# Two output products computed in pairs of chunks, with seven block products for eight in two steps of each pair

## The chip, the cores and the metric

The kernel runs on one core of one Trainium2 chip. The metric is the device time of one execution, in microseconds (us), as the median of several executions. The names used here: PE is TensorE (matmuls; PEld its weight loads), DVE is VectorE, ACT is ScalarE, POOL is GpSimd, SP is the engine whose queue issues the weight stream's transfers.

## What is computed

The reference is two transformer layers on 256 tokens of width 2048, all in float32. Only the two products that the change touches matter in detail:

```python
def hybrid_layer(x, ...):
    ...
    y = jax.nn.sigmoid(g_a) * y_a + jax.nn.sigmoid(g_b) * y_b
    return x + jnp.einsum('bsd,de->bse', y, w_out)          # first output product, 256x2048 by 2048x2048

def second_block(x, norm_mix_g, w_in, w_fourier, w_out, norm_mlp_g, w_up, w_down, norm_final_g):
    h = x
    u = _rmsnorm(h, norm_mix_g[layer])
    ...                                                      # Fourier mixing and attention give y_f and y_a
    y = jnp.concatenate([y_f, y_a], axis=-1)
    h = h + jnp.einsum('bse,ed->bsd', y, w_out[layer])       # second output product, the same size
    u = _rmsnorm(h, norm_mlp_g[layer])
    a = jnp.square(jax.nn.relu(jnp.einsum('bsd,df->bsf', u, w_up[layer])))
    h = h + jnp.einsum('bsf,fd->bsd', a, w_down[layer])
    return _rmsnorm(h, norm_final_g)
```

The results have to be close to float32, so every product is made from three matmuls in the chip's fp32r type: high part by high part, high by low, low by high.

## The kernel before

**The stream of weights.** All weights lie in one DRAM array, `stream`, in units of 128 by 2048 floats (1 MB). SP loads unit u into one of four places of `raw` as soon as the unit four back has been split. A unit is used in *pieces*. ACT rounds a piece to its high part (`w_hi`, L1154), DVE subtracts to get the low part (`w_lo`, L1665), PE multiplies with both. The places of `w_hi` and `w_lo` form a ring of four pieces (six in the last stage, the MLP). ACT and DVE run the same loop as PE: at position k (after PE has used piece k) they split piece k+4 into the freed place, and then do what else is written for position k, which the code calls its *slot*. So whatever stands in a slot on DVE delays the later splits and everything else behind it on that engine; each engine works its own list strictly in order, and engines meet only at semaphores.

**A plain product.** `project` (L593 to L595) makes one chunk, 512 columns of the result, for both halves of the tokens, in two PSUM banks: 8 pieces, 12 matmuls each. The two output products are four such chunks each: w_out from about 1017 to 1108 us, w_out_2 from about 1330 to 1422 us of the profile. After each chunk DVE adds the residual in `add_chunk` (L2202, results in `nat`).

**Turning.** The next stage needs the result with features on the partitions: for each of eight groups PE transposes four 128x128 blocks (L566) into a bank, ACT writes the high part (L1186), DVE the low part (L1709 with a norm's weight, L1705 without). The function `turn` places them: six groups (`tail`) after pieces 1 to 6 of the product's last chunk, one per piece, two (`head`) after pieces 2 and 3 of the next stage. Two banks alternate, so a group waits until DVE has read the group two before it.

**A pair with sums.** Other products (the pairs in the input stage, 160 to 458 us, and in the MLP) already use the scheme that the change brings here. `pair_in` works on two chunks at a time, so on four banks (`whole`), in eight steps of 2x2 blocks (two blocks of the inner dimension, two of the columns, times two halves of tokens). `plain_step` is 8 block products in two pieces. `sum_step` is 7 block products (the Winograd form of Strassen's scheme) in four pieces, and adds into four more banks (`mixed`). For it DVE makes sums of weight blocks ahead (`sum_weights`, L1679, L1682, L1683; this is done right after the first piece of the unit *before* the sum unit has been split) and sums of the activations' blocks once (`sum_x`, L1856 to L1862). The second `sum_step` of a pair is step 4 or 5 of 0 to 7. After the step behind it DVE joins the mixed banks: `join_mixed` part 0 in the first slot and part 1 in the second slot of that step (L1919 to L1924), then `join_whole` (L1936) as the last step's four products end. All eight banks are in use, so the next pair, whose `whole` is this pair's `mixed`, cannot start before `join_mixed` has ended; PE waits for `part_read`.

## Time and profile before

| what | us |
|---|---|
| median of 3 executions | 2123.62 (2123.57 to 2124.18) |
| the profiled execution | 2124.27 |
| its span, first to last instruction | 2122.4 |
| outside the span | 1.9 |
| PE busy | 2098.2 |
| DVE busy | 1447.1 |
| ACT busy | 1082.3 |

The granted TensorE clock was 1.00 in all stages shown below (2.4 GHz). A row of the timeline gives start, duration, engine, line, operation and tiles, and in brackets how long the engine idled before and what released it. "Matmuls are pipelined": a PE row's 0.39 us is a latency, and the pace is the distance of two starts.

### The profile page before, as it was taken

Reading aid. Unit: us, or ns where it says so; the run is one execution under the profiler, and the core shown is the slowest. Engines: PE = TensorE matmul, PEld = TensorE weight load, DVE = VectorE, ACT = ScalarE, POOL = GpSimd, SP = SyncE. Lnnn points to the kernel's source line nnn. Section 1 sums busy time; section 2 is a strip of 40 time slices with the busy share of each in tenths; the row PEclk is TensorE's granted clock in tenths of the full one; section 3 lists DMA queues with packets and bytes.
Section 4 is the critical chain, followed back from the end, with each engine's and each line's share of the span. In section 5 each row is a group of like instructions: output and inputs, shape, how many; then the busy total and the mean of one; then the engine's idle time right before and its main releaser. Section 6 shows DMA issues by size and latency. Waiting matters only on the chain.

```text
span 2122.4 us, 24939 instructions
## 1 busy us (share of the span) xinstructions
PE 2098.2 (99%) x10067; PEld 1752.8 (83%) x10067; DVE 1447.1 (68%) x1868; ACT 1082.3 (51%) x1392; POOL 37.9 (2%) x49
## 2 busy tenths in 40 slices
PE   8999999999999999999999999999999999999998
PEld 6888888888888877788888888888888888888886
DVE  5877788875555776556554455466896796797684
ACT  5545555555444674454455444355544554454553
POOL 0000000000000020000000000000000000000000
PEclk9999999999999999999999999999999999999999
DMA  7555555565465544355755442455555465546452
GB/s 266 184 181 196 199 189 208 185 248 181 178 223 189 188 154 156 122 220 197 296 188 184 180 170 107 142 207 187 193 202 186 172 224 193 180 187 227 180 218 98
DMA packets 56563, 402.60 MB, mean 190 GB/s; under 512 B 6240, under 2 KB 6496, under 8 KB 9216
## 3 DMA queue, kind: packets, MB, share of 16 engines
q1 hardware_dynamic: 53648, 380.67, 50.1%
q0 software_dynamic: 2656, 19.81, 2.4%
q8 instruction: 80, 1.31, 0.2%
q10 hardware_dynamic: 144, 0.52, 0.1%
q14 instruction: 35, 0.29, 0.0%
HBM read 392.59 MB, written 8.39 MB: 189 GB/s over the span
## 4 chain that ended last, share of the span: by engine, by line
PE 96%; DVE 1%; ACT 1%; issue 1%; DMA 0%; SPq 0%; POOLq 0%; POOL 0%; DVEq 0%; ACTq 0%
PE proj L593 15%; PE proj L595 15%; PE proj L594 15%; PE proj L1048 11%; PE proj L1051 6%; PE proj L698 4%; PE proj L699 4%; PE proj L700 4%; PE tbank L698 2%; PE tbank L699 2%; PE tbank L700 2%; PE tbank L566 2%; PE bank_a L698 1%; PE bank_a L700 1%; PE bank_a L699 1%; PE bank_b L698 1%
## 5 line engine op out<-in xcount | busy, mean ns | idle before, releaser
L1665 DVE TENSOR_TENSOR w_lo<-raw,w_hi 128x1024 fp32r<-128x1024 f32 x630 | 749.4, 1200 | 528.6 <-ACT w_hi L1154 521.5
L1154 ACT ACTIVATE w_hi<-raw 128x1024 fp32r<-128x1024 f32 x630 | 652.1, 1041 | 770.3 <-PE proj L595 495.1
L593 PE MATMUL proj<-w_hi,a_both 128*128 128x512 f32 x1280 | 512.2, 400 | 0.0
L595 PE MATMUL proj<-w_hi,a_both 128*128 128x512 f32 x1280 | 499.8, 390 | 0.0
L594 PE MATMUL proj<-w_lo,a_both 128*128 128x512 f32 x1280 | 498.4, 389 | 0.0
L595 PEld LDWEIGHTS proj<-w_hi,a_both 128*128 128x128 f32 x1280 | 240.2, 188 | 51.7
L593 PEld LDWEIGHTS proj<-w_hi,a_both 128*128 128x128 f32 x1280 | 240.5, 188 | 51.1 <-issue 4.3
L594 PEld LDWEIGHTS proj<-w_lo,a_both 128*128 128x128 f32 x1280 | 240.7, 188 | 47.5
L1048 PE MATMUL proj<-a_both,w_hi 128*128 128x512 f32 x672 | 168.4, 392 | 0.3 <-DVE a_both L1709 0.3
L1048 PEld LDWEIGHTS proj<-a_both,w_hi 128*128 128x128 f32 x672 | 121.0, 189 | 22.2 <-DVE a_both L1709 0.5
L1154 ACT ACTIVATE w_hi_deep<-raw 128x1024 fp32r<-128x1024 f32 x84 | 85.7, 1025 | 94.1 <-PE proj L1051 57.6
L1665 DVE TENSOR_TENSOR w_lo_deep<-raw,w_hi_deep 128x1024 fp32r<-128x1024 f32 x84 | 98.1, 1178 | 42.6 <-ACT w_hi_deep L1154 42.3
L1051 PEld LDWEIGHTS proj<-a_both,w_lo 128*128 128x128 f32 x672 | 91.7, 190 | 6.5
L1051 PE MATMUL proj<-a_both,w_lo 128*128 128x256 f32 x672 | 93.7, 282 | 0.0
L1048 PE MATMUL proj<-a_both,w_hi_deep 128*128 128x512 f32 x352 | 88.1, 392 | 0.0
L1048 PEld LDWEIGHTS proj<-a_both,w_hi_deep 128*128 128x128 f32 x352 | 63.4, 189 | 11.4
L698 PE MATMUL proj<-w_hi,a_both 128*128 128x512 f32 x164 | 64.0, 391 | 0.4 <-DVE w_lo L1665 0.4
L700 PE MATMUL proj<-w_hi,a_both 128*128 128x512 f32 x164 | 63.8, 389 | 0.0
L699 PE MATMUL proj<-w_lo,a_both 128*128 128x512 f32 x164 | 63.8, 389 | 0.0
L1051 PEld LDWEIGHTS proj<-a_both,w_lo_deep 128*128 128x128 f32 x352 | 48.0, 190 | 3.4
L1051 PE MATMUL proj<-a_both,w_lo_deep 128*128 128x256 f32 x352 | 49.1, 282 | 0.0
L593 PE MATMUL proj<-w_hi,lat_hi 128*128 128x512 f32 x112 | 45.6, 407 | 0.4 <-DVE v_b L2164 0.4
(511 smaller groups left out, 2997.0 us busy)
## 6 DMA issues: line engine op xcount, KB each, us to landing
raw<-stream SPq DMA_DIRECT2D x359, 1024.0 KB, 4.8
nat<-x SPq DMA_DIRECT2D x4, 512.0 KB, 9.0
z_store<-z POOLq DMA_DIRECT2D x1, 2048.0 KB, 8.2
ga_store<-z POOLq DMA_DIRECT2D x1, 2048.0 KB, 11.4
gb_store<-z POOLq DMA_DIRECT2D x4, 512.0 KB, 7.0
yb<-z_store POOLq DMA_DIRECT2D x4, 512.0 KB, 7.7
ga<-ga_store POOLq DMA_DIRECT2D x1, 2048.0 KB, 8.2
gb<-gb_store POOLq DMA_DIRECT2D x1, 2048.0 KB, 14.7
```

The source lines that it names most:

```text
L566: last = nc.tensor.transpose(tbank[tr.n % 2][:, b * P:(b + 1) * P], src(b), ident)
L593: nc.tensor.matmul(banks[t][:, :], ah, wh, start=first, stop=False)
L594: nc.tensor.matmul(banks[t][:, :], ah, wl, start=False, stop=False)
L595: last = nc.tensor.matmul(banks[t][:, :], al, wh, start=False, stop=end)
L698: nc.tensor.matmul(bank[:, :], hi, wh, start=first, stop=False)
L699: nc.tensor.matmul(bank[:, :], hi, wl, start=False, stop=False)
L700: return nc.tensor.matmul(bank[:, :], lo, wh, start=False, stop=end)
L1048: nc.tensor.matmul(banks[f], hi_places[s][:, cols], a_both[:, kt, :, :].rearrange("p s t -> p (s t)"), start=(kt == 0), stop=False)
L1051: last = nc.tensor.matmul(banks[f][:, 0:TOK], lo_places[s][:, cols], a_hi[:, kt, :], start=False, stop=(kt == KT - 1))
L1154: A(hi_places[s][:, 0:width], src, ACT.Copy).then_inc(w_rounded, 1)
L1665: V.tensor_tensor(lo_places[s][:, 0:width], src, hi_places[s][:, 0:width].bitcast(f32), SUB).then_inc(w_rest, 1)
```

## The change

Both output products are now two pairs of chunks each, numbered r = 0, 1 (w_out) and 2, 3 (w_out_2), each like `pair_in`: 8 steps, of which two are sum steps, at steps 3 and 5 (r=0), 2 and 5 (r=2), 1 and 4 (r=1 and 3). A pair has 20 pieces, numbered here 0 to 19 for the first pair of a stage and 20 to 39 for the second. The sum units of r=1 and r=3 are the second of the pair, so their weights' sums follow the split of piece 20, which falls on position 16 of the pair before.

- `sum_y` and `rest_of_y_sums` make the activations' sums in positions 0, 2, 3 and 5 of the stage, on DVE (ACT rounds them in `round_y_sums`).
- `add_mixed_out` is `join_mixed` with four additions more at the end of part 1 (the residual, all four tiles), and both parts stand in the two slots of the step behind the second sum step. `add_whole_out` adds the four whole banks and writes `nat`; `res_ready` counts these.
- The turning moves: PE's groups 0 to 3 come two by two after each piece of step 6 of the second pair, 4 and 5 after the pair, 6 and 7 after the next stage's first piece. They use two banks of the pair's `mixed` (`turn_banks`), so the first also waits for `add_mixed_out` part 1.
- The squares for the norm (`res_squares`, ACT) move with the results. The weights' units are laid out in the new order. The number of units is the same.

```diff
+            def pair_out(r, before, slot):                     # PE
+                whole, mixed = parts_out[r // 2][r % 2], parts_out[r // 2][1 - r % 2]
+                at, f = SUM_AT_OUT[r], r // 2
+                if r % 2:
+                    pe.wait_ge(part_read, READ_OUT + r)
...
+                for step in range(STEPS):
+                    g = ORDER_OUT[r][step]
+                    if step == at[0]:
+                        if r % 2:
+                            pe.wait_ge(res_ready, 8 * f + 4)
...
+                    if step in at:
+                        i = at.index(step)
+                        sum_step(2 * g, whole, mixed, a_hi, a_lo, yo_hi[f][:, i], yo_lo[f][:, i], 2 + 2 * f + i + 1, i == 0,
+                                 i == len(at) - 1)
+                    elif step == STEPS - 1:
+                        end_step(2 * g, whole, a_hi, a_lo, END_OUT)
+                    else:
+                        plain_step(...)
...
+            def turn_out(f):                                   # PE
+                def put(g):
+                    if not first:
+                        first.append(by_dve.n)
+                        pe.wait_ge(part_read, READ_OUT + 2 * f + 2)
+                    pe.wait_ge(res_ready, 8 * f + (4 if g < 4 else 6 if g < 6 else 8))
+                    group(from_nat(nat, g), by_dve, banks=turn_banks[f])
+                def tail(step, h):
+                    if step == 6:
+                        put(2 * h)
+                        put(2 * h + 1)
...
-            projection(y_head, y_before, r_tail)
+            pair_out(0, y_before, lambda step, h: y_head(2 + h) if step == 1 else None)
+            pair_out(1, None, r_tail)
+            r_put(4)
+            r_put(5)
...
-            projection(mix_slot, mix_before, m_tail)
+            pair_out(2, mix_before, lambda step, h: mix_slot(0) if step == 0 and h == 0 else None)
+            pair_out(3, None, m_tail)
+            m_put(4)
+            m_put(5)
...
+            def add_mixed_out(r, part):                        # DVE
+                if part == 0:
+                    dve.wait_ge(m_copied, PAIRS_IN + r + 1)
+                    chain(V.tensor_tensor(m[:, 2, :], mixed[2][:, :], m[:, 0, :], ADD))
+                    chain(V.tensor_tensor(m[:, 1, :], mixed[1][:, :], m[:, 2, :], ADD))
+                if part == 1:
+                    chain(V.tensor_tensor(m[:, 2, :], mixed[3][:, :], m[:, 2, :], ADD))
+                    V.tensor_tensor(m[:, 3, :], mixed[1][:, :], m[:, 2, :], ADD).then_inc(part_read, 1)
...
+                    for o in range(4):
+                        t, cols = part_out(r, o)
+                        last = V.tensor_tensor(m[:, o, :], other[:, t, cols], m[:, o, :], SUB if o in (1, 2) else ADD)
...
+            def pair_out(r, side):                             # DVE
+                    def slot(j):
+                        side(step, j)
+                        if r % 2 == 0:
+                            if (step, j) in ((0, 0), (1, 1)):
+                                sum_y(f, step)
+                            if (step, j) in ((1, 0), (2, 1)):
+                                rest_of_y_sums(f, step - 1)
+                        if step == at[-1] + 1:
+                            add_mixed_out(r, j)
+                        if r % 2 and step == 6:
+                            turned(f, 2 * j)
+                            turned(f, 2 * j + 1)
```

**Where the order of work changes.** First place: DVE at the start of the w_out product. The first row is the split of the stage's piece 3; L2188 to L2196 (L2301 to L2309 after) are the gating of the last chunk of the stage before. Before:

```order
L1665 TENSOR_TENSOR w_lo<-raw,w_hi 128x1024
L2188 TENSOR_TENSOR nat<-nat,stg 128x512 x2
L2193 TENSOR_TENSOR stg_126<-proj,stg_126 128x512
L2196 TENSOR_TENSOR nat<-nat,stg_126 128x512
L2193 TENSOR_TENSOR stg_126<-proj,stg_126 128x512
L2196 TENSOR_TENSOR nat<-nat,stg_126 128x512
L1665 TENSOR_TENSOR w_lo<-raw,w_hi 128x1024 x3
L1705 TENSOR_TENSOR a_both<-tbank,a_both 128x2x256
L1665 TENSOR_TENSOR w_lo<-raw,w_hi 128x1024
L1705 TENSOR_TENSOR a_both<-tbank,a_both 128x2x256
L1665 TENSOR_TENSOR w_lo<-raw,w_hi 128x1024 x4
```

After (from the last gating row on; L1792 to L1796 are the sums of weights, L2318 to L2329 those of the activations, `w_lo` is L1778 now):

```order
L2309 TENSOR_TENSOR nat<-nat,stg_134 128x512
L1778 TENSOR_TENSOR w_lo<-raw,w_hi 128x1024
L1792 TENSOR_TENSOR w_sum_mix<-raw 128x1024
L1795 TENSOR_TENSOR w_sum_mix<-w_sum_mix,raw 128x512
L1796 TENSOR_TENSOR w_sum_mix<-w_sum_mix,raw 128x512
L2318 TENSOR_TENSOR stg<-a_both 128x512
...
L1778 TENSOR_TENSOR w_lo<-raw,w_hi 128x1024 x2
L1818 TENSOR_TENSOR a_both<-tbank,a_both 128x2x256
L2329 TENSOR_TENSOR y_lo<-stg,y_hi 128x512
L1778 TENSOR_TENSOR w_lo<-raw,w_hi 128x512
L1818 TENSOR_TENSOR a_both<-tbank,a_both 128x2x256
L2318 TENSOR_TENSOR stg<-a_both 128x512
```

Between the splits of pieces 4, 5, 6 and 7 stand now three weight sums and twice the five operations of `sum_y`, where nothing stood but the low parts of two turned groups.

Second place: DVE at the change from r=0 to r=1 (the same stands at r=2 to r=3). Before, at the end of a chunk:

```order
L1705 TENSOR_TENSOR a_both<-tbank,a_both 128x2x256
L1665 TENSOR_TENSOR w_lo<-raw,w_hi 128x1024 x4
L2202 TENSOR_TENSOR nat<-proj,yb 128x512 x2
L1665 TENSOR_TENSOR w_lo<-raw,w_hi 128x1024 x8
L2202 TENSOR_TENSOR nat<-proj,yb 128x512 x2
```

After (the first row ends with piece 20, split in position 16; the row before the last is piece 22):

```order
L1778 TENSOR_TENSOR w_lo<-raw,w_hi 128x1024 x5
L1792 TENSOR_TENSOR w_sum_mix<-raw 128x1024
L1795 TENSOR_TENSOR w_sum_mix<-w_sum_mix,raw 128x512
L1796 TENSOR_TENSOR w_sum_mix<-w_sum_mix,raw 128x512
L2348 TENSOR_TENSOR added_mix<-tbank,added_mix 128x512
L2349 TENSOR_TENSOR added_mix<-proj,added_mix 128x512
L1778 TENSOR_TENSOR w_lo<-raw,w_hi 128x1024
L2351 TENSOR_TENSOR added_mix<-tbank,added_mix 128x512
L2352 TENSOR_TENSOR added_mix<-proj,added_mix 128x512
L2359 TENSOR_TENSOR added_mix<-yb,added_mix 128x512 x4
...
L1778 TENSOR_TENSOR w_lo<-raw,w_hi 128x1024
L1778 TENSOR_TENSOR w_lo<-raw,w_hi 128x512
```

Where lines are left out stand the four additions of the whole banks (L2371). Two additions between two chunks have become three weight sums, four joins, four residual additions and four additions of whole banks, with one split among them.

Third place: DVE at the turning, in the last chunk or pair of the product. Before, low parts come one group (two operations) per split:

```order
L1665 TENSOR_TENSOR w_lo<-raw,w_hi 128x1024 x2
L1709 SCALAR_TENSOR_TENSOR a_both<-tbank,par,a_both 128x256 x2
L1665 TENSOR_TENSOR w_lo<-raw,w_hi 128x1024
L1709 SCALAR_TENSOR_TENSOR a_both<-tbank,par,a_both 128x256 x2
L1665 TENSOR_TENSOR w_lo<-raw,w_hi 128x1024
```

After, they stand two by two behind the joins:

```order
L2348 TENSOR_TENSOR added_mix<-proj,added_mix 128x512
L2349 TENSOR_TENSOR added_mix<-bank_b,added_mix 128x512
L1778 TENSOR_TENSOR w_lo<-raw,w_hi 128x1024
L2351 TENSOR_TENSOR added_mix<-proj,added_mix 128x512
L2352 TENSOR_TENSOR added_mix<-bank_b,added_mix 128x512
L2359 TENSOR_TENSOR added_mix<-yb,added_mix 128x512 x4
L1778 TENSOR_TENSOR w_lo<-raw,w_hi 128x1024
L1822 SCALAR_TENSOR_TENSOR a_both<-bank_a,par,a_both 128x256 x2
L1822 SCALAR_TENSOR_TENSOR a_both<-bank_b,par,a_both 128x256 x2
```

The transposes moved from one group per piece to two per piece, and the joins stand ahead of them.

## Rows read from the trace of the kernel before

**Rows 1.** The page: busy us (share) and instructions of each engine
```profile
PE 2098.2 (99%) x10067; PEld 1752.8 (83%) x10067; DVE 1447.1 (68%) x1868; ACT 1082.3 (51%) x1392; POOL 37.9 (2%) x49
```

**Rows 2.** Busy us by window: PE, PEld, DVE, ACT, POOL, clock, DMA share, GB/s
```profile
372.00:415.00 43.00, 43.00 (x192) 35.59 (x191) 36.21 (x40) 22.98 (x25) 0.00 (x0) 1.00 0.54 199
1017.00:1108.00 91.00, 91.00 (x419) 75.27 (x417) 52.54 (x59) 44.18 (x60) 2.31 (x4) 1.00 0.66 252
1330.00:1422.00 92.00, 92.00 (x419) 76.20 (x418) 49.78 (x56) 43.94 (x59) 0.00 (x0) 1.00 0.49 172
```

**Rows 3.** Who waited for whom: total us, times, longest us
```profile
PE proj L698 <- DVE w_lo L1665: 0.4, 1, 0.4
...
PE proj L1048 <- DVE a_both L1709: 0.3, 1, 0.3
```

**Rows 4.** Timeline of PE in w_out_2 and in w_out: start us, duration us, engine, line
```profile
1334.48 0.40 PE L594 MATMUL proj<-w_lo,a_both 128*128 128x512 f32 x1
...
1402.04 0.39 PE L595 MATMUL proj<-w_hi,a_both 128*128 128x512 f32 x1
...
1025.48 0.60 PE L566 MATMUL tbank<-cst,nat 128*128 128x128 f32 x4
...
1028.70 0.60 PE L566 MATMUL tbank<-cst,nat 128*128 128x128 f32 x4
```

**Rows 5.** Timeline of DVE, a pair of the input stage, around a weight sum
```profile
307.41 1.23 DVE L1665 TENSOR_TENSOR w_lo<-raw,w_hi 128x1024 fp32r<-128x1024 f32 x1
308.55 1.22 DVE L1679 TENSOR_TENSOR w_sum_vo<-raw 128x1024 f32<-128x1024 f32 x1
...
311.14 2.96 DVE L1665 TENSOR_TENSOR w_lo<-raw,w_hi 128x1024 fp32r<-128x1024 f32 x3
```

**Rows 6.** Timeline of PE, the same pair, at its wait for that split
```profile
312.42 0.50 PE L698 MATMUL proj<-w_hi,a_both 128*128 128x512 f32 x1
312.75 0.39 PE L699 MATMUL proj<-w_lo,a_both 128*128 128x512 f32 x1
```

**Rows 7.** Timeline of ACT and of PE at the same pair's last step
```profile
325.67 1.06 ACT L1154 ACTIVATE w_hi<-raw 128x1024 fp32r<-128x1024 f32 x1 [1.11 <-PE proj L700]
...
325.47 0.39 PE L698 MATMUL proj<-w_hi,a_both 128*128 128x512 f32 x1
...
330.91 0.39 PE L698 MATMUL bank_a<-w_hi,a_both 128*128 128x512 f32 x1
```

**Rows 8.** Timeline of DVE, the same pair, its joins
```profile
325.25 0.68 DVE L1919 TENSOR_TENSOR joined<-tbank,joined 128x512 f32<-128x512 f32 x1
325.97 0.69 DVE L1920 TENSOR_TENSOR joined<-bank_b,joined 128x512 f32<-128x512 f32 x1
326.77 1.23 DVE L1665 TENSOR_TENSOR w_lo<-raw,w_hi 128x1024 fp32r<-128x1024 f32 x1
327.91 0.68 DVE L1923 TENSOR_TENSOR joined<-tbank,joined 128x512 f32<-128x512 f32 x1
328.63 0.69 DVE L1924 TENSOR_TENSOR joined<-bank_b,joined 128x512 f32<-128x512 f32 x1
329.42 2.49 DVE L1936 TENSOR_TENSOR joined<-proj,joined 128x512 f32<-128x512 f32 x4
```

**Rows 9.** Timeline of DVE, sums of the activations in the input stage
```profile
89.29 0.69 DVE L1856 TENSOR_TENSOR x_whole<-a_both 128x512 f32<-128x512 f32 x1
...
91.07 1.22 DVE L1665 TENSOR_TENSOR w_lo<-raw,w_hi 128x1024 fp32r<-128x1024 f32 x1
```

**Rows 10.** Timeline of DVE at the start of the w_out stage
```profile
1020.13 1.29 DVE L2188 TENSOR_TENSOR nat<-nat,stg 128x512 f32<-128x512 f32 x2
...
1023.99 2.35 DVE L1665 TENSOR_TENSOR w_lo<-raw,w_hi 128x1024 fp32r<-128x1024 f32 x2
```

**Rows 11.** Timeline of DVE: a turned group's low part; the last Fourier group's in w_out_2
```profile
1404.70 0.87 DVE L1709 SCALAR_TENSOR_TENSOR a_both<-tbank,par,a_both 128x256 fp32r<-128x256 f32 x2
...
1335.09 0.69 DVE L2267 TENSOR_TENSOR a_both<-bank_b,a_both 128x512 fp32r<-128x512 f32 x1
```

More of the change, by code:

```diff
@@ L59 @@
 SUM_UNITS = _sum_units()
-SUMS_IN = 2 * PAIRS_IN
 def _pieces():
@@ L1474, in res_squares @@
                     square_sum(stg2[:, t, :], nat[:, t, c * CW:(c + 1) * CW], ss2[:, t, c:c + 1])
-            for c in range(4):
-                def slot(j, c=c):
-                    if c == 0:
-                        turn_head(j)
-                    if c == 3:
-                        turn_tail(j, "mix_g")
-                    if c and j == 3:
-                        res_squares(c - 1, 2 * c)
-                pieces(slot=slot)
-                chunk.add()
+            pair_out(0, lambda step, j: turn_head(2 + j) if step == 1 else None)
+            pair_out(1, lambda step, j: None)
             for i in range(4):
@@ L1553, in _ @@
                     mapped(g)
-            for c in range(4):
-                def slot(j, c=c):
-                    if c == 0 and j == 0:
-                        mapped(FG - 1)
-                    if c == 3:
-                        turn_tail(j, "mlp_g")
-                    if c and j == 3:
-                        res_squares(c - 1, 8 + 2 * c)
-                pieces(slot=slot)
-                chunk.add()
+            pair_out(2, lambda step, j: mapped(FG - 1) if step == 0 and j == 0 else None)
+            pair_out(3, lambda step, j: None)
             def round_hidden(c):
@@ new lines, in pair_out, with slot @@
+            def pair_out(r, side):
+                at, f = SUM_AT_OUT[r], r // 2
+                for step in range(STEPS):
+                    def slot(j):
+                        side(step, j)
+                        if r % 2 == 0:
+                            if (step, j) in ((0, 0), (1, 1)):
[5 more added lines that the diff above has]
+                        if r % 2 and step == 6:
+                            turned(f, 2 * j)
+                            turned(f, 2 * j + 1)
+                        if r % 2 and step == 7 and j == 0:
+                            turned(f, 4)
+                            turned(f, 5)
+                    if step == STEPS - 1:
+                        add_whole_out(r)
+                    pieces(4 if step in at else 2, slot=slot)
+                chunk.add(2)
@@ L2215, in mean_of_chunks @@
+            pair_out(0, lambda step, j: turn_head(2 + j) if step == 1 else None)
+            pair_out(1, lambda step, j: None)
             def mean_of_chunks(n):
@@ L2285, in _ @@
                     mapped(g)
-            for c in range(4):
-                pieces(slot=(lambda j: mapped(FG - 1) if j == 0 else None) if c == 0 else
-                       (lambda j: turn_tail(j, "mlp_g")) if c == 3 else None)
-                add_chunk(c, nat)
+            pair_out(2, lambda step, j: mapped(FG - 1) if step == 0 and j == 0 else None)
+            pair_out(3, lambda step, j: None)
             def rest_of_hidden(c):
```

205 lines of the change are left out of this document (155 added, 50 removed).

## The prediction

> **What bounds the kernel now.** I read the busy shares first: PE is busy 99% of the span, DVE 68%, ACT 51% [rows 1]. In the two stages that change PE is busy in every microsecond of the windows, at the full clock, DVE in 52.5 of 91 and 49.8 of 92 us [rows 2]. Then the list of waits: PE hardly ever waits for DVE; the two entries that matter here are 0.4 us on a low part of weights in a pair and 0.3 us on a turned group as the MLP begins [rows 3]. So PE's matmul count is the time, as long as DVE hands over in time. The question is whether a ring of four pieces still hides DVE once the pairs' extra work is on it. A pair of the input stage keeps DVE busy 36.2 of 43 us [rows 2], so its slack is small and local order matters; that is why the timelines come last and carry the sum.
>
> **The gain.** From 1334.48 to 1402.04 lie 298 steps of one matmul: 0.227 us each [rows 4]. A product is three matmuls, 0.68; a plain piece 12, 2.73; a plain step 5.46; a sum step 21, 4.78 in pieces of 1.36, 0.68, 1.36, 1.36. Each of 8 sum steps drops one product, three matmuls: 24 x 0.2275 = 5.46 us. The 16 groups of transposes stay; one costs PE 0.49, since a piece with one takes 3.22 from start to start [rows 4]. The number of weight units, and so the transfers, stays too.
>
> **The clockwork of the ring.** ACT starts 0.20 to 0.26 us after PE leaves a piece (325.47 to 325.67 [rows 7]) and takes 1.06, DVE follows 0.04 later with 1.23. So a low part four pieces ahead is ready about 2.6 us after PE leaves a piece, if DVE is free; in a row of ready work the next DVE operation starts after 1.14 (326.77 to 327.91). Half-width operations follow each other after 0.72 when chained (325.25 to 325.97 [rows 8]), after 0.61 when not (two in 1.29 [rows 10]). Three weight sums take 2.59 (308.55 to 311.14 [rows 5]), the activations' sums 1.78 (89.29 to 91.07 [rows 9]), a turned group's low part 0.80 to 0.87 [rows 11]. After a wait PE loses 0.11 more, since the first matmul takes 0.33 to the next [rows 6].
>
> The Trainium skill, VectorE: DVE Perf Modes, section "The DRAIN you can't avoid", says that the next operation does not start until the pipe is empty and that a semaphore in between costs nothing. The rows differ: 0.61 without, 0.72 with a chain. By the rule all eight unchained additions per pair change would be 0.11 longer, 0.9 us each at two places; the rows are taken.
>
> **Cost A, start of w_out.** DVE is free of the last gating at 1023.99 [rows 10]. Now follow: split 4, weight sums (from 1025.13), `sum_y` (1027.72), splits 5 and 6 (1029.50, 1030.64), low part of group 6, rest of the sums, split 7, group 7, `sum_y` (1034.2) and split 8 from 1036.0 to 1037.25. PE leaves the second transposes at 1029.2 (1028.70 + 0.49 [rows 4]), is at the sum step's first piece at 1034.65 and wants piece 8 at 36.7: it waits 0.6. ACT must round the second sums first (36.1 to 36.7), so split 9 ends at 38.93: 0.2. Split 10 ends at 40.7: 0.3. Then the second weight sums, and split 11 ends at 44.4, where PE wants it at 43.6: 0.9. With four restarts 2.4 us. The last of these waits exists already in the input pairs, 0.4 [rows 3, 6], which checks the method: same place, less work ahead. Ends: 0.4 and 4.
>
> **Cost A', start of w_out_2.** DVE comes out of the Fourier part idle, so only `mapped` (0.69 [rows 11]) and the two sums lie ahead. PE's piece 1 begins at 1334.25 (one matmul ahead of the first of [rows 4]), so piece 3 is left at 1342.4, its position's split 7 lets `sum_y` begin at 1344.9 and split 8 at 1346.6, ready at 1347.8; three pieces and a sum step bring PE there at 1347.2. With the restart 0.8. The first weight sums fall into the last Fourier-input chunk, behind which the Fourier part's small matmuls use no pieces; they cost nothing.
>
> **Cost B, change of pairs (r=0 to 1, 2 to 3).** I lay the new list on the pair at 325 us. There split 20 ends at 325.3, joins end at 329.3, and PE passes to the next pair at 330.91 unhindered [rows 7, 8]. Now 2.59 of weight sums come in at 325.25, both joins of part 0 end the chain at 329.3, split 21, and the last join ends at 331.85. PE waits for `part_read` until 331.9: 1.0. Then four residual additions (2.5), four whole additions (2.5, from 334.4), split 22 from 337.0 to 338.2. PE has two pieces, 5.46 us, and wants piece 22 at 337.45: 0.8. Restarts 0.2. Sum 2.0, twice: 4.0. Behind it splits 23 to 27 are ready 0.3 us and more ahead. Split 20 started there only when ACT had rounded piece 20, so DVE was waiting and lateness from A is gone by then. In `pair_in` the next weight sum comes only after the change, so the trace shows no such wait. Ends: 1.0 and 3.0 each.
>
> **Cost C, turning (r=1 and 3).** Let PE leave step 5 at Q. The second slot gives: ACT to Q+1.3, split 39 to 2.6, joins to 3.9. In the pair at 325 the same took 329.32 - 325.47 = 3.85 [rows 7, 8], unseen, since nobody asked before 5.46. Now PE asks after one piece, at 2.73, for its first transposes: 1.2. Then DVE has four residual additions (to 6.5), split 40 (to 7.7), and the low parts of groups 0 and 1, ready at 8.5 and 9.3. PE has put groups 0 and 1 by 4.9 and used piece 37 by 7.7, and needs those two banks free again for groups 2 and 3: 0.9 and 0.3. At the end groups 6 and 7 need 4 and 5 read: 0.1. Sum 2.5, twice: 5.0. Before, one group came per piece, with nothing else on DVE but the split. Ends: 1.2 and 3.4 each.
>
> **MLP start.** After r=3 the low part of group 7 is ready at about 10.4 us behind the pair's end, when PE reaches the piece that needs it; the present 0.3 [rows 3] goes. ACT's squares move by a few us and have two chunks' time.
>
> **Sum.** -5.46 + 2.4 + 0.8 + 4.0 + 5.0 - 0.3 = +6.4 us. The profiled execution took 2124.27, which is 0.65 above the median; 2124.27 + 6.4 = 2130.7, on the scale of the medians **2130.0**.
>
> **Rivals.** (1) *The ring hides it: faster.* DVE has 35 to 40 us idle in each stage [rows 2]; if ACT and DVE catch up, only the 0.4 us wait remains, once per stage: -5.46 + 0.8 = -4.7, 2118.9. It decides at C: the last join must end within 2.73 us of Q, where the trace shows 3.85. Against it speaks that number, and that B puts 13 us of DVE work between the splits 20 and 22, with only split 21 inside. The Trainium skill, Perfetto Trace Analysis, section "Identifying the Most-Contended Engine", advises work on the engine with the highest occupancy, which is PE; by that rule the full 5.46 comes back. The page's shares agree on who is busiest, but not on who hands over late. (2) *The waits swallow one another.* Each stall gives DVE time. If A vanishes in the gating's slack and B or C loses its second wait (0.8, 1.2), the costs are 12.2 - 3.2 - 2 x 1.2 = 6.6: +0.8 to +3.5, 2124.4 to 2127. (3) *Dearer.* Additions at 0.72 throughout (+0.9 in each B, +0.4 in each C), or weights landing late, because the sums want their unit one step sooner while POOL's own transfers run: +2 to +4, 2132 to 2134. (4) That the change doesn't do what it says: the order of PE's instructions shows 24 matmuls fewer of these kinds, so no chance is kept for it.
>
> **How the numbers follow.** Forecast 0.62 (2127.5 to 2132), dearer 0.12, swallowed 0.18, hidden 0.08. Range 2126 to 2134: of the swallowed case it takes in the upper third, of the others all but the hidden. What a measurement of this kernel can tell from no change is 0.2%, 4.2 us: faster is below 2119.4, slower above 2127.9. Slower 0.62 x 0.95 + 0.12 = 0.71; faster, the hidden case, where 2118.9 lies just past the line, 0.06; same the rest, 0.23.
>
> **What would show it.** In the new profile: the waits list should name PE waiting for DVE's join (`added`) twice before a pair and twice before transposes, about 1 us each; for `w_lo` twice in the second pair's first sum step, and four times around the first pair's sum steps; for low parts at the third and fourth transposes. PE's busy time falls by 5 us while the span grows. If the waits list is as short as before, the ring hid it. If PE's total waiting in 1017 to 1110 is below 4 us, A or C was mis-sized. Wrong outright would be a DVE list that runs ahead of its slots.

## The result, and the profile after

| what | before | after |
|---|---|---|
| median | 2123.69 us (2123.48 to 2124.18) | 2131.84 us (2131.24 to 2132.06) |
| span of the profiled execution | 2122.4 us | 2130.1 us |
| PE busy | 2098.2 us | 2095.7 us |
| DVE busy | 1447.1 us | 1507.1 us |

The ratio is 1.0038, with a 95% interval of 1.0027 to 1.0048: slower by 8.15 us, a small step but clear of the scatter, where 6.4 were forecast. The engines' line of the changed kernel answers to [rows 1], the windows to [rows 2] (the end of each is shifted by the delay up to there; the columns are PE, PEld, DVE, ACT, POOL, clock, DMA share, GB/s):

```profile
PE 2095.7 (98%) x10043; PEld 1746.7 (82%) x10043; DVE 1507.1 (71%) x1964; ACT 1097.5 (52%) x1416; POOL 37.8 (2%) x49
```

```profile
1017.00:1113.00 96.00, 90.53 (x404) 72.23 (x404) 81.53 (x104) 48.34 (x64) 2.30 (x4) 1.00 0.63 239
1330.00:1427.00 97.00, 91.48 (x416) 74.63 (x415) 76.34 (x100) 48.10 (x62) 0.00 (x0) 1.00 0.44 158
```

PE has 24 matmuls fewer and the clock is the full 1.00, so the gain was delivered. But where PE was busy in every microsecond, it now idles for 5.5 of 96 us and 5.5 of 97 us, and DVE went from 52.5 and 49.8 us to 81.5 and 76.3 us. Over the whole windows DVE is at 85 and 79%, so the shares still name PE as the fullest. The list of waits says who hands over late (engine, tile and line that waited, who was waited for, total us, times, longest us):

```profile
PE proj L721 <- DVE w_lo L1778: 2.5, 4, 0.9
PE bank_a L721 <- DVE w_lo L1778: 2.1, 4, 0.9
...
PE bank_a L589 <- DVE added_mix L2352: 1.1, 1, 1.1
PE proj L589 <- DVE added_two L2352: 1.1, 1, 1.1
PE proj L589 <- DVE a_both L1822: 1.1, 2, 0.9
...
PE bank_a L589 <- DVE a_both L1822: 0.9, 1, 0.9
...
PE bank_a L721 <- DVE added_two L2352: 0.8, 1, 0.8
PE proj L721 <- DVE added_mix L2352: 0.8, 1, 0.8
...
PE bank_b L589 <- DVE a_both L1822: 0.2, 1, 0.2
```

In [rows 3] there was one such entry of 0.4 us for `w_lo` (it is still in the first line here). No entry for the two products names a transfer. The entry for the MLP's start (`a_both`, 0.3 us) is gone.

Idle time in these rows is counted from the modelled end of the matmul before. To set waits against the forecast I use the distance between two starts, less the pace of 0.23 us per matmul. These PE rows show the reading, for each kind of place; the bracket names who released PE:

```profile
1037.55 0.50 PE L721 MATMUL proj<-w_hi,y_hi 128*128 128x512 f32 x1 [0.55 <-DVE w_lo L1778]
1037.89 0.40 PE L722 MATMUL proj<-w_lo,y_hi 128*128 128x512 f32 x1
...
1064.22 0.50 PE L721 MATMUL proj<-w_hi,a_both 128*128 128x512 f32 x1 [0.81 <-DVE added_mix L2352]
1064.56 0.39 PE L722 MATMUL proj<-w_lo,a_both 128*128 128x512 f32 x1
...
1100.77 0.66 PE L589 MATMUL bank_a<-cst,nat 128*128 128x128 f32 x4 [1.09 <-DVE added_mix L2352]
...
1105.56 0.63 PE L589 MATMUL bank_a<-cst,nat 128*128 128x128 f32 x4 [0.92 <-DVE a_both L1822]
1106.34 0.63 PE L589 MATMUL bank_b<-cst,nat 128*128 128x128 f32 x4 [0.16 <-DVE a_both L1822]
```

The matmul ahead of 1064.22 started at 1063.03, so PE lost 1.19 - 0.23 = 0.97 us there, and 0.11 more to the restart (64.22 to 64.56 is 0.34 where 0.23 is the pace). Of two groups of transposes in a row the second starts 0.50 us after a first that waited (1100.77 to 1101.27) and 0.43 after one that didn't (1112.28 to 1112.71); what is above that is the second's own wait, 0.78 - 0.50 = 0.28 at 1106.34. All waits of the two products, measured so:

| place | w_out | w_out_2 | forecast |
|---|---|---|---|
| turned group 7, at 1034.64 | 0.30 | none | none |
| A: pieces 8, 9, 10, 11 at 1037.55, 1039.29, 1041.12, 1044.75 | 0.71, 0.25, 0.34, 0.82 | - | 0.6, 0.2, 0.3, 0.9 |
| A': piece 8 of w_out_2, at 1353.20 | - | 0.88 | 0.8 with its restart |
| B: join before the second pair, at 1064.22 and 1380.78 | 0.97 | 0.97 | 1.0 |
| B: piece 22, at 1070.84 and 1387.41 | 1.05 | 1.05 | 0.8 |
| C: join before the transposes, at 1100.77 and 1417.33 | 1.25 | 1.25 | 1.2 |
| C: banks of groups 2 and 3, from 1105.56 and 1422.11 | 1.08, 0.28 | 1.08, 0.28 | 0.9, 0.3 |
| C: bank of group 7, at 1116.57 | 0.24 | none | 0.1 each |
| restarts, 0.03 to 0.11 each | 0.9 | 0.4 | 4 x 0.11, then 0.2 per B |
| sum, less 12 matmuls (2.73) | 8.2 - 2.7 = 5.4 | 5.9 - 2.7 = 3.2 | 4.2 and 2.6 |

Landmarks confirm it. The last transposes before the w_out product start at 1014.13 us before and 1013.86 after; the first transposes of the fourth stage, well behind that product, at 1136.40 and 1141.54: 0.3 us ahead there and 5.1 behind here, so 5.4 us lie between, as the table has it. From the last Fourier group (1324.62 and 1329.76) to the last matmul of the program (2114.14 and 2121.81) the delay grows by 2.5 us: the second product's 3.2 less what is saved at the MLP's start. There 0.58 us are gone, since the steps from the first turned groups to the end of the second piece behind them took 7.04 us (1427.05 to 1434.09) and take 6.46 (1432.50 to 1438.96). So the table gives 2.6. Together it has 5.4 + 3.2 - 0.6 = 8.0 us. The spans differ by 7.7 (2122.4 and 2130.1), because the profiled execution of the changed kernel was 0.3 us ahead before the first product began.

### The profile page after: what moved, and what is told of

Read it like the earlier page. It is cut to its first block, busy times and chain, and to the rows that moved or that the text cites. A ratio compares the mean times of both kernels' runs of the same rounds, so it can differ in the third digit from the quotient of the medians.

```text
span 2130.1 us, 25043 instructions
## 1 busy us (share of the span) xinstructions
PE 2095.7 (98%) x10043; PEld 1746.7 (82%) x10043; DVE 1507.1 (71%) x1964; ACT 1097.5 (52%) x1416; POOL 37.8 (2%) x49
## 4 chain that ended last, share of the span: by engine, by line
PE 91%; DVE 4%; ACT 2%; issue 1%; DMA 0%; SPq 0%; POOLq 0%; POOL 0%; DVEq 0%; ACTq 0%
PE proj L616 12%; PE proj L618 12%; PE proj L617 12%; PE proj L1142 11%; PE proj L1145 6%; PE proj L721 5%; PE proj L723 5%; PE proj L722 5%; PE tbank L721 3%; PE tbank L723 3%; PE tbank L722 3%; PE tbank L589 2%; PE bank_a L721 2%; PE bank_a L723 1%; PE bank_a L722 1%
## 5 line engine op out<-in xcount | busy, mean ns | idle before, releaser
L1778 DVE TENSOR_TENSOR w_lo<-raw,w_hi 128x1024 fp32r<-128x1024 f32 x630 | 742.5, 1193 | 462.4 <-ACT w_hi L1248 455.3
L616 PE MATMUL proj<-w_hi,a_both 128*128 128x512 f32 x1024 | 411.0, 401 | 0.0
L618 PE MATMUL proj<-w_hi,a_both 128*128 128x512 f32 x1024 | 400.0, 391 | 0.0
L617 PE MATMUL proj<-w_lo,a_both 128*128 128x512 f32 x1024 | 398.7, 389 | 0.0
L616 PEld LDWEIGHTS proj<-w_hi,a_both 128*128 128x128 f32 x1024 | 192.4, 188 | 41.6 <-issue 4.3
L618 PEld LDWEIGHTS proj<-w_hi,a_both 128*128 128x128 f32 x1024 | 192.2, 188 | 41.4
L617 PEld LDWEIGHTS proj<-w_lo,a_both 128*128 128x128 f32 x1024 | 192.6, 188 | 37.9
L1778 DVE TENSOR_TENSOR w_lo_deep<-raw,w_hi_deep 128x1024 fp32r<-128x1024 f32 x84 | 98.0, 1178 | 40.7 <-ACT w_hi_deep L1248 40.3
L721 PE MATMUL proj<-w_hi,a_both 128*128 128x512 f32 x272 | 107.0, 393 | 3.0 <-DVE w_lo L1778 2.0
L723 PE MATMUL proj<-w_hi,a_both 128*128 128x512 f32 x272 | 105.9, 389 | 0.0
L722 PE MATMUL proj<-w_lo,a_both 128*128 128x512 f32 x272 | 105.9, 389 | 0.0
L721 PEld LDWEIGHTS proj<-w_hi,a_both 128*128 128x128 f32 x272 | 51.0, 188 | 15.8 <-issue 2.4
L721 PE MATMUL tbank<-w_hi,a_both 128*128 128x512 f32 x156 | 60.8, 390 | 0.0
L723 PE MATMUL tbank<-w_hi,a_both 128*128 128x512 f32 x156 | 60.7, 389 | 0.0
```

The lines of the kernel that those rows point to most:

```text
L616: nc.tensor.matmul(banks[t][:, :], ah, wh, start=first, stop=False)
L617: nc.tensor.matmul(banks[t][:, :], ah, wl, start=False, stop=False)
L618: last = nc.tensor.matmul(banks[t][:, :], al, wh, start=False, stop=end)
L721: nc.tensor.matmul(bank[:, :], hi, wh, start=first, stop=False)
L722: nc.tensor.matmul(bank[:, :], hi, wl, start=False, stop=False)
L723: return nc.tensor.matmul(bank[:, :], lo, wh, start=False, stop=end)
```

## The experiments

**The theory.** DVE works its list strictly in order. At three places of each output product the list is denser than PE's time for it: weight sums (2.59 us), joins, residual additions (2.5), whole additions (2.5). DVE falls behind there and PE pays the difference. **The rivals**: the lag is only carried to the next dense place when work is moved, so that moving it wins nothing; or the waits have another cause (transfers, banks, clock), which moving DVE's work would not touch. Transfers and the clock can be set aside at once: in no run does the waits list name a transfer in the two products, and the clock was 1.00 in both windows of the changed kernel. Most experiments change one table: `SUM_AT_OUT` says at which steps of the four pairs the sum steps stand (with the order of blocks that belongs to it); this moves weight sums, joins and all that hangs on them. The kernel before was timed anew beside each group of runs, with medians of 2124.0 us (e1 to e4), 2123.9 (e5 to e8) and 2123.61 (e12, e13), and the ratios go by these. The changed kernel's 2131.84 stands beside 2123.69, so a distance from it is good to 0.3 us.

### The odd pairs' first sum step later, and earlier joins

```diff
-SUM_AT_OUT = [(3, 5), (1, 4), (2, 5), (1, 4)]
+SUM_AT_OUT = [(3, 5), (2, 4), (2, 5), (2, 4)]    # e1_first_later
+SUM_AT_OUT = [(3, 5), (1, 3), (2, 5), (1, 3)]    # e2_second_earlier
+SUM_AT_OUT = [(3, 5), (2, 3), (2, 5), (2, 3)]    # e3_both
```

> The changed kernel, with the first sum step of the second pair of each product at step 2 instead of step 1 (2,4 for 1,4). Theory (order of DVE's list): the weight sums for it then fall behind the change of pairs, so both waits there vanish (0.97 for the joins and 1.05 for the next low part, with restarts 2.2 us at each of two places), the waits at the turning (2.5 each) stay, and a wait of up to 0.36 us appears on the plain step between the sum steps, as the input pairs have it: 8.15 - 4.4 + 0.7 = +4.4 against the kernel before, about 2128.1. Rival (DVE has too much work in the stage as a whole, wherever it stands): the waits move and the sum stays, 2131 to 2132.5.

Measured: 2131.75 us (2131.11 to 2132.01), 1.0036 of before (1.0023 to 1.0049). PE passes to the second pair unhindered: the starts around 1064 follow each other at 0.23. But two new waits, and one of 0.19, stand later in each product, and C is as it was. Rows of PE:

```profile
1071.92 0.50 PE L724 MATMUL proj<-w_hi,a_both 128*128 128x512 f32 x1 [0.46 <-DVE w_lo L1781]
...
1083.44 0.50 PE L724 MATMUL proj<-w_hi,a_both 128*128 128x512 f32 x1 [0.67 <-DVE w_lo L1781]
```

and DVE's list just ahead of the first:

```profile
1066.91 1.23 DVE L1781 TENSOR_TENSOR w_lo<-raw,w_hi 128x1024 fp32r<-128x1024 f32 x1
1068.06 1.22 DVE L1795 TENSOR_TENSOR w_sum_mix<-raw 128x1024 f32<-128x1024 f32 x1
1069.31 0.69 DVE L1798 TENSOR_TENSOR w_sum_mix<-w_sum_mix,raw 128x512 f32<-128x512 f32 x1
1070.03 0.69 DVE L1799 TENSOR_TENSOR w_sum_mix<-w_sum_mix,raw 128x512 f32<-128x512 f32 x1
1070.64 2.95 DVE L1781 TENSOR_TENSOR w_lo<-raw,w_hi 128x1024 fp32r<-128x1024 f32 x3
```

By distances of starts the waits are 0.62, 0.19 and 0.83, together 1.6 with 0.3 for restarts, against the 2.0 and 0.2 that went: 0.3 us less in each product. The time above the kernel before is 7.75 us where it was 8.15: the whole move is worth 0.4 us, where 3.7 were expected. The weight sums left the place ahead of the join, and arrive at a place where DVE is still behind. My expectation fell, and the rival (the lag is carried on) is right for this move.

> The changed kernel, with the second sum step of the second pair of each product at step 3 instead of step 4 (1,3 for 1,4). Theory: the joins and the residual additions are done a whole step before the first transposes, so the waits at the turning go (1.25, 1.08 and 0.2 us at each of two places, 5.1 us in all), the waits at the change of pairs stay, and the 0.36 us on the step between may appear: 8.15 - 5.1 + 0.7 = +3.8, about 2127.5. Rival (too much DVE work as a whole): 2131 to 2132.5.

Measured: 2127.99 us (2127.53 to 2128.44), 1.0019 (1.001 to 1.0028), 3.85 us below the changed kernel. C's waits are gone from both products, but for group 3's, which stays at 0.25 in w_out. B stays (0.97 and 1.04); 0.21 and 0.19 are new. This is a real gain because the joins, now in step 4, end before PE asks for their banks in step 6: DVE is done with the additions behind them at 1098.25, and the first transposes start at 1099.86.

> The changed kernel, with the sum steps of the second pairs at 2 and 3 (2,3 for 1,4): both moves at once. Theory: waits at the change of pairs and at the turning both go (9.5 us together), only the waits in the first pairs stay (about 3.2 and 1.0 us), two sum steps in a row may cost up to 1 us: 2122.3 to 2123.5, level with or just below the kernel before. Rival (too much DVE work as a whole): two sum steps in a row ask DVE for 13 us of work in 9.6 us of PE's, and the total stays near 2131. Second rival (the pair form costs PE something by itself, for example by its bank order): not below 2126 even with no wait left.

Measured: 2125.55 us (2125.34 to 2126.22), 1.0008 (0.9999 to 1.0017): 2 to 3 us above what I expected. The join's wait is gone, and C but for group 3's 0.25 in w_out. Behind the change of pairs remain 0.63, 0.18, 0.27 and 0.30 in each product. With two sum steps next to each other their weight sums follow at a distance of one step, while DVE still works off joins and additions. So C is removable and B is not: it is split up.

### Only the residual additions

```diff
-                    for o in range(4):                       # in add_mixed_out, part 1, all pairs
-                        t, cols = part_out(r, o)
-                        last = V.tensor_tensor(m[:, o, :], other[:, t, cols], m[:, o, :], SUB if o in (1, 2) else ADD)
-                    chain(last)
+                    if r % 2 == 0:                           # e4_late_adds; e7_no_adds has nothing here
+                        add_rest_out(r)
...
                         if r % 2 and step == 6:
                             turned(f, 2 * j)
                             turned(f, 2 * j + 1)
+                            if j:
+                                add_rest_out(r)
```

> The changed kernel, with the four residual additions of the second pairs put behind the low parts of turned groups 2 and 3 instead of ahead of those of 0 and 1; the work is the same. Theory: the first wait at the turning (1.25 us, for the joins) stays, the second and third (1.08 and 0.2, for banks that DVE has not read) go, 1.3 at each of two places: 8.15 - 2.6 = +5.6, about 2129.3. Rival (too much DVE work as a whole): the whole additions become late instead and hold the next stage's transposes, no change, 2131 to 2132.

Measured: 2131.48 us (2131.21 to 2131.54), 1.0035 (1.0022 to 1.0048). C's second and third wait are gone, and a new one stands behind the pair, where PE wants to transpose its results:

```profile
PE bank_a L589 <- DVE nat L2377: 1.4, 1, 1.4
...
PE proj L589 <- DVE nat L2377: 0.5, 1, 0.5
```

```profile
1107.57 0.87 DVE L1822 SCALAR_TENSOR_TENSOR a_both<-bank_b,par,a_both 128x256 fp32r<-128x256 f32 x2
1108.35 2.49 DVE L2347 TENSOR_TENSOR added_mix<-yb,added_mix 128x512 f32<-128x512 f32 x4
1110.87 0.69 DVE L2377 TENSOR_TENSOR nat<-proj,added_mix 128x512 f32<-128x512 f32 x1
...
1112.22 0.66 PE L589 MATMUL bank_a<-cst,nat 128*128 128x128 f32 x4 [1.38 <-DVE nat L2377]
```

The same 2.49 us stand now straight ahead of the additions that PE waits for. The rival was right again, but for a rest: the distance from the kernel before is 7.5 us where it was 8.15, so the move is worth about 0.7 us.

> The changed kernel without the four residual additions of each pair, 16 DVE operations of 0.61 us left out; the output lacks these terms. Theory: DVE is 2.5 us earlier at each change of pairs and each turning. The waits for the joins stay (0.97 and 1.25), the second ones go (1.05, and 1.08 with 0.2; with restarts 2.4 at each of two places): -4.9, about 2127. Rival (the lag sits in the joins and weight sums alone): nothing, 2131 to 2132.

Measured: 2127.0 us (2126.22 to 2127.42), 1.0014 (1.0005 to 1.0024), 4.8 us below the changed kernel, with the residual missing from the result. B's join wait (0.97) and C's first (1.25) stay to the hundredth; B's wait for piece 22 and C's for the banks of groups 2 and 3 are gone. That is 2 x (1.05 + 1.08 + 0.28) = 4.8 us and restarts. So two kinds of waits are told apart. The first of each place is the joins' own lateness. The second is the 2.5 us of additions behind the joins. Only here, where the work is taken away and not moved, is the whole price of the term seen.

### The first pairs' sum steps, and all together

```diff
-SUM_AT_OUT = [(3, 5), (1, 4), (2, 5), (1, 4)]
+SUM_AT_OUT = [(4, 5), (1, 4), (4, 5), (1, 4)]    # e5_even_later
+SUM_AT_OUT = [(4, 5), (2, 3), (4, 5), (2, 3)]    # e6_all
+SUM_AT_OUT = [(4, 5), (2, 3), (2, 4), (2, 3)]    # e8_mixed
```

> The changed kernel, with the sum steps of the first pairs at 4 and 5 (4,5 for 3,5 and for 2,5). Theory (DVE carries a lag from where its list is dense to where PE asks): the first stage's start gets a whole plain step before the first weight sums are wanted, so of its five waits (2.4 us and 0.5 of restarts, with the one for the turned group) only about 0.7 stays, and the 0.9 at the second product goes: 8.15 - 3.3 = +4.9, about 2128.6. The waits at the change of pairs and at the turning stay as they are. Rival (the lag is only carried on, as the run with 2,4 in the second pairs suggests): the waits come again at the change of pairs, 2131 to 2132.

Measured: 2128.96 us (2128.71 to 2129.72), 1.0025 (1.0015 to 1.0035), 2.9 us below the changed kernel. A is down to 0.24 and 0.88, A' is gone, B and C are unchanged. As the theory has it, DVE has time to work off the gating, the activations' sums and the turned groups before the first sum step.

> 4,5 in the first pairs and 2,3 in the second pairs. Theory: the savings of the two single moves add up, since DVE waits for PE once in between: 6.3 of the run with 2,3 and 3.3 of the run with 4,5, 2131.84 - 9.6 = 2122.2, 1.5 to 2 us below the kernel before. Rival (the lag is carried on): no better than the run with 2,3 alone, 2125.5.

Measured: 2123.3 us (2122.72 to 2123.49), 0.9998 (0.9988 to 1.0007): no difference from before that can be measured. The waits list still has 1.2 us for `w_lo` in the first product. Waits by distances of starts are 0.24, 0.88, 0.63, 0.20, 0.28, 0.27 in the first product and the last four in the second; groups 3 and 7 wait 0.25 each in w_out. With 1.0 for restarts that is 2.50 + 1.38 + 0.5 + 1.0 = 5.4 us, against 5.46 us of matmuls and 0.58 at the MLP: -0.6 worked out, -0.6 measured. DVE at the remaining place:

```profile
1058.54 0.68 DVE L2354 TENSOR_TENSOR added_mix<-tbank,added_mix 128x512 f32<-128x512 f32 x1
...
1060.10 2.50 DVE L2362 TENSOR_TENSOR added_mix<-yb,added_mix 128x512 f32<-128x512 f32 x4
1062.63 0.69 DVE L2374 TENSOR_TENSOR nat<-bank_a,added_mix 128x512 f32<-128x512 f32 x1
...
1071.26 1.22 DVE L1795 TENSOR_TENSOR w_sum_mix<-raw 128x1024 f32<-128x1024 f32 x1
```

Here stand, from 1057.40 to 1078.6 us, the second part of the join, eight additions, twice three weight sums (the second from 1071.26) and nine splits. The window's DVE column reads 20.70 of 21.20 us:

```profile
1057.40:1078.60 21.20, 20.58 (x89) 16.09 (x87) 20.70 (x25) 9.92 (x17) 0.00 (x0) 1.00 0.44 153
```

For these 21 us DVE is the bound, and all four waits behind the change of pairs lie in or just behind them.

> 4,5 and 2,3 in the first product, 2,4 and 2,3 in the second: against the run with 4,5 and 2,3 in both it has the joins of the third pair one step sooner. Theory: of the waits that the run with 2,3 still has behind the change of pairs (0.6, 0.2, 0.3, 0.3 and restarts, 1.8 us) those of the second product go, and two sum steps with one plain step between cost up to 0.9: 2121 to 2122.2. Rival: two sum steps that close carry their lag on, 2123 or more.

Measured: 2124.15 us (2123.84 to 2124.79), 1.0003 (0.9993 to 1.0013). In w_out_2 the earlier sum steps bring waits of 0.89 and 0.78 at 1348.07 and 1351.70, and in the second pair 0.19 and 0.67 stand where e6_all has four waits of together 1.38. The rival was right: the lag was carried, here forward in time, and (4, 5) is the better place.

### The weight sums on POOL

DVE is the late one and POOL is busy for 2% of the span [rows 1]. Both kernels have this edit, the second with the positions of e6_all; SP also waits for a unit's sums before it loads over the unit (not shown):

```diff
+            def sum_weights(i):                              # POOL, for the 8 sum units of the output products
+                u = SUM_UNITS[i]
+                pool.wait_ge(w_rest, FIRST_PIECE[u - 1])
+                pool.wait_ge(raw_landed[u % RING], (u // RING + 1) * 16)
...
+                nc.gpsimd.tensor_tensor(s[:, 0:2, :], b[:, 0:3:2, :], b[:, 3, :].unsqueeze(1).to_broadcast([P, 2, CW]),
+                                        ALU.add).then_inc(w_summed, 1)
+                nc.gpsimd.tensor_tensor(s[:, 2, :], s[:, 0, :], b[:, 2, :], ALU.add).then_inc(pool_seq, 1)
+                nc.gpsimd.tensor_tensor(s[:, 3, :], s[:, 2, :], b[:, 1, :], ALU.add).then_inc(w_summed, 1)
...
-                    if u + 1 in SUM_UNITS and piece.n == FIRST_PIECE[u]:
+                    if u + 1 in SUM_UNITS and piece.n == FIRST_PIECE[u] and not SUMS_IN <= SUM_UNITS.index(u + 1) < SUMS_OUT:
```

> The changed kernel with the 8 weight sums of the output products (three operations each) on POOL instead of DVE; the sum steps stand as in the changed kernel. Theory (DVE's list is what is late): 2.59 us leave DVE's list at each sum step, so the waits at the starts of both products go (3.7 and 0.9 with restarts) and those at the change of pairs (2.2 each), the turning's stay (2.5 each): 8.15 - 9 = -0.8, 2122.8 to 2124. Unknown: what such an operation takes on POOL, which no trace here shows; up to twice DVE's time it is hidden, since a unit lands two units before its use. Rival (POOL is slow, or slows DVE's own reads of the same memory): ACT waits for the sums, or DVE's splits grow from 1.23, and the time is 2128 or more.

Measured: 2133.91 us (2133.42 to 2135.22), 1.005 (1.0033 to 1.0067), 2 us above the changed kernel, and about 10 above what I expected. The rival was right. B's join wait falls to 0.26, piece 22's (1.03), A' (0.88) and C stay, and PE now waits up to 2.5 us (at 1044.52) for low parts. The reason is in the rows of POOL and DVE beside each other:

```profile
1025.10 2.41 POOL L576 TENSOR_TENSOR w_sum_mix<-raw 128x1024 f32<-128x1024 f32 x1
1027.60 1.42 POOL L579 TENSOR_TENSOR w_sum_mix<-w_sum_mix,raw 128x512 f32<-128x512 f32 x1
...
1024.97 2.70 DVE L2345 TENSOR_TENSOR stg<-stg 128x128 f32<-128x128 f32 x1
1027.60 0.28 DVE L2346 TENSOR_TENSOR stg<-stg 128x128 f32<-128x128 f32 x1
1027.91 1.26 DVE L2347 TENSOR_TENSOR stg<-stg 128x128 f32<-128x128 f32 x1
...
1040.97 7.85 DVE L1802 TENSOR_TENSOR w_lo<-raw,w_hi 128x1024 fp32r<-128x1024 f32 x3
...
1060.91 0.68 DVE L2372 TENSOR_TENSOR added_mix<-tbank,added_mix 128x512 f32<-128x512 f32 x1
```

A DVE operation of 0.28 us takes 2.70 us when POOL works on a sum beside it, and ends 0.16 us behind POOL's; the next, recorded from the moment POOL's second begins, takes 0.28; the third again lasts until 0.15 behind POOL's. Later three splits in a row take 7.85 us where three take 3.5 without POOL; the first of them takes 3.4, and its end at 1044.37 releases PE from the longest wait. The last row is a join, which reads one of its two inputs from a PSUM bank: it takes its usual 0.68 us though POOL works on a sum from 1059.98 for 2.17 us. So the 2.59 us that were taken off DVE's list come back as time in which DVE stands still, and POOL needs more of it: the three sums take about 2.5 + 2.0 + 1.7 us in w_out (a 128x512 one between 1.29 and 2.17):

```profile
L576 POOL TENSOR_TENSOR w_sum_mix<-raw 128x1024 f32<-128x1024 f32 x4 | 10.0, 2489 | 34.3 <-DVE w_lo L1802 34.2
...
L579 POOL TENSOR_TENSOR w_sum_mix<-w_sum_mix,raw 128x512 f32<-128x512 f32 x4 | 7.9, 1974 | 0.3
```

The Trainium skill states this in SBUF — State Buffer, section "SBUF: two separate sides": GpSimd and a DVE operation with two SBUF inputs share a pair of ports as an exclusive lock, and whoever holds it blocks the other for a whole instruction. The trace agrees, with the durations above; one row departs from it, since the operation of 1024.97 is recorded as starting 0.13 us ahead of POOL's and still ends behind it. My expectation had this only as its rival (DVE's splits grow), without a price for it.

> 4,5 in the first pairs and 2,3 in the second, and the weight sums on POOL. Theory: no wait is left in either product, so the 24 matmuls come back whole: 2123.9 - 5.5 - 0.3 = 2118.2, to 2119.5. Rival (POOL slow or in DVE's way): two sum steps in a row want 6 operations within 5 us of PE, and ACT waits for them: 2123 or more.

Measured: 2134.44 us (2133.07 to 2135.07), 1.0049 (1.0034 to 1.0064), 11 us above e6_all; the rival was right again. The waits for low parts grow to 3.0 us at 1042.81 and 2.7 us at 1071.85 and 1389.65. Behind the latter two something else appears, here in rows of PE and in three windows (columns as in [rows 2]):

```profile
1071.85 0.73 PE L748 MATMUL proj<-w_hi,a_both 128*128 128x512 f32 x1 [2.52 <-DVE w_lo L1805]
...
1072.79 0.63 PE L750 MATMUL proj<-w_hi,a_both 128*128 128x512 f32 x1
1073.22 0.63 PE L748 MATMUL proj<-w_hi,a_both 128*128 128x512 f32 x1
```

```profile
1068.00:1071.80 3.80, 1.33 (x6) 0.75 (x4) 3.65 (x6) 0.63 (x1) 0.00 (x0) 1.00 0.00 0
1071.80:1075.40 3.60, 3.55 (x9) 2.82 (x10) 3.60 (x3) 0.00 (x0) 2.39 (x1) 0.53 0.36 100
1075.40:1080.00 4.60, 4.60 (x22) 3.78 (x21) 2.88 (x2) 1.77 (x2) 4.44 (x3) 1.00 0.85 294
```

Starts follow at 0.43 us instead of 0.23, and the windows give the granted clock: 1.00, then 0.53 for 3.6 us, then 1.00 (0.56 from 1389.60 to 1393.20). That is the lower of the two levels, 1.2 GHz, for most of the stretch. Eight matmuls at 0.43 instead of 0.23 cost 1.6 us at each of the two places. The length of the wait alone does not decide it: behind the 3.0 us at 1042.81 in the same kernel, and behind the 2.5 us at 1044.52 in e12_pool_sums, the next starts follow at 0.23 and the clock is 1.00. What tells these places apart stays open. Behind the waits of 1.5 us and less in the two products the starts follow at 0.23 in every run.

## Why the prediction was right, and where its sizes were off

**Bound.** PE's matmul count is the time as long as DVE hands over in time: confirmed. The page has exactly 24 matmuls fewer, and the time rose by the waits. PE's busy time fell by 2.5 us, not by the 5 that I had named as a sign. At a wait the matmul before it counts as busy for 0.16 us beyond the pace (0.81 us idle in the bracket for a wait of 0.97), and the restart counts too, so busy time understates what was saved.

**The gain, 5.46 us.** It came in full. e6_all shows it: with 5.4 us of waits left, and 0.58 saved at the MLP's start, the kernel stands level with the one before.

**A, 2.4 us.** Its four waits were 0.71, 0.25, 0.34 and 0.82, with four restarts 2.56 us. Missed was one ahead of them: turned group 7, 0.30 and a restart. The rows of the changed kernel:

```profile
1030.96 1.23 DVE L1778 TENSOR_TENSOR w_lo<-raw,w_hi 128x1024 fp32r<-128x1024 f32 x1 [0.51 <-ACT w_hi L1248]
...
1033.91 0.68 DVE L1818 TENSOR_TENSOR a_both<-tbank,a_both 128x512 fp32r<-128x512 f32 x1
...
1034.64 0.50 PE L721 MATMUL proj<-w_hi,a_both 128*128 128x512 f32 x1
```

The working had DVE go from split 5 straight to split 6 (1030.64), be done with group 7 when `sum_y` begins at 1034.2, and PE arrive at 1034.65, so no wait. But ACT rounds the first sums at 1029.35, as soon as DVE has made them, and only then piece 6, from 1029.88. So split 6 waits 0.51 us for ACT, and group 7's low part ends at 1034.59, behind PE's arrival at 1034.34. The working had this rounding for the second sums and left it out for the first. **A'** was forecast as 0.8 and is 0.96. e5_even_later takes most of A and all of A' away by giving DVE time before the first sum step, as the mechanism wants.

**B, 2.0 us each.** The join's wait is 0.97 where 1.0 stood. The one for piece 22 is 1.05 where 0.8 stood: this term is mis-sized. The rows of the changed kernel, DVE's and then PE's, give the reason:

```profile
1063.47 0.69 DVE L2352 TENSOR_TENSOR added_mix<-proj,added_mix 128x512 f32<-128x512 f32 x1
1064.31 2.50 DVE L2359 TENSOR_TENSOR added_mix<-yb,added_mix 128x512 f32<-128x512 f32 x4
...
1068.64 0.68 DVE L2371 TENSOR_TENSOR nat<-proj,added_mix 128x512 f32<-128x512 f32 x1
1069.47 1.83 DVE L1778 TENSOR_TENSOR w_lo<-raw,w_hi 128x1024 fp32r<-128x1024 f32 x2
...
1070.84 0.47 PE L721 MATMUL bank_a<-w_hi,a_both 128*128 128x512 f32 x1 [0.89 <-DVE w_lo L1778]
```

The working had 5.15 us from the last join's end to the start of the split (331.85 to 337.0), and PE going on the moment the split ends. Here the join ends at 1064.16, the additions begin 0.15 later, and from the start of the last one to the split 0.83 pass instead of 0.60: 5.31 in all. The split of piece 22, the first and full-width one of the two in that row, takes 1.23, so it ends at 1070.70, and PE starts 0.14 later. Against the working's unrounded 0.75 (338.2 - 337.45) 0.30 us are missing: 0.16 are gaps on DVE, 0.14 is PE's start behind the split. Both gaps stand where the code lets DVE wait for its own last operation and then signal another semaphore (`sem_inc`). I had costed them as plain steps, though a gap like them stands in the working's own rows (328.63 to 329.42 is 0.79 [rows 8]).

**C, 2.5 us each.** 1.25, 1.08 and 0.28 for 1.2, 0.9 and 0.3, with 0.15 of restarts that the sum had left out. The small one at the end is 0.24 in w_out, where 0.1 stood, and absent in w_out_2. e7_no_adds shows that the division was right: without the additions the 1.25 stays and the others go.

**MLP start.** Forecast as 0.3 saved, by the idle time in the bracket. By the distance of starts it is 0.58, with the restart.

**The sum.** The terms as measured add up to 8.0 us where 6.4 were forecast. Of these 1.6 us, 0.4 is group 7 with its restart, 0.4 B (2 x 2.2 against 2 x 2.0), 0.2 A', 0.1 A and 0.8 C, less 0.3 at the MLP. The mechanism held at every place that the working named, one wait (group 7) was not named, and the forecast is low because nearly all its sizes were low. The medians differ by 8.15, which the 8.0 explain; the spans of the two profiled executions differ by only 7.7, for the 0.3 told above.

**What follows an operation on DVE.** On "The DRAIN you can't avoid" in VectorE: DVE Perf Modes, of the Trainium skill (a semaphore in between costs nothing, measured there on eight copies), the trace of the changed kernel disagrees as that of before did: unchained additions follow after 0.60, chained ones after 0.72, and where DVE also signals another semaphore after 0.83. This last price makes up the 0.16 us of gaps in B's second wait. By the rule of "Identifying the Most-Contended Engine" in the Trainium skill's Perfetto Trace Analysis (rival 1) 5.46 us would have come back; the time rose by 8.15 us.

**The rivals.** (1) *Hidden by the ring* is refuted: C's first wait is 1.25 where it should have vanished. (2) *Waits swallow one another* did not occur in the changed kernel, every wait of B and C stands in full in both products. Its mechanism, a stall that gives DVE time, is still real, seen the other way round: in e1_first_later the join's wait, taken away at the first piece of the pair, came back as 0.62 at its fourth. (3) *Dearer* comes close to the right total (its 2132 to 2134 begins just above 2131.84) for wrong reasons: the additions took 0.60 to 0.63, not 0.72, and no wait names a transfer of weights. (4) is refuted by the count of matmuls. The range, 2126 to 2134, holds the time.

## What to carry to other kernels

Read the busy share of a helper engine in the stretch of one or two pieces, not of the stage: DVE at 71% of the span was full for 21 us at a time in e6_all, and 24 matmuls saved (5.46 us) cost 13.5 us of waits (8.2 and 5.9 in the two products, less 0.6 at the MLP). Before moving work off a dense place, ask whether the engine has caught up where it is put. Moves that only carried the lag to another place won at most 0.7 us (e1_first_later, e4_late_adds) or lost (e8_mixed against e6_all), while those that let the work end before PE's next question (e2_second_earlier, e5_even_later) won most of its price.

## What the runs showed of the hardware

- DVE's operations with two SBUF inputs stand still while POOL adds tensors in SBUF (fp32, 128x512 and 128x1024): 0.28 us became 2.70, and three splits of 3.5 us together became 7.85, while a join with one input in PSUM kept its 0.68. Work moved from DVE to POOL was dearer than on DVE, with DVE working beside it: 2.49 us for 128x1024 against 1.22, and 1.7 to 2.0 for 128x512 (1.28 at the least) against 0.69.
- Behind two waits of 2.7 us PE's granted clock was 0.53 and 0.56 for 3.6 us, at 0.43 us per matmul; behind waits of 2.5 and 3.0 us elsewhere it stayed at 1.00.
- A wait of PE in the two products costs 0.07 to 0.12 us more than its own length, in the distance from the first matmul to the second (0.30 to 0.35 instead of 0.23). A group of transposes costs the matmul behind it 0.09 in the same way, with no wait (1025.88 and 1029.10).
